# The query blocks of a decoder's channel mixer as products of split halves

## The reference

```python
h   = RMSNorm(x) * (1 + scale2) + shift2
q   = (h @ w_q).reshape(T, 8 heads, 2 halves, 128)
s1  = einsum('thd,nd->thn', q[:, :, 0], key1)      # 128 keys
s2  = einsum('thd,nd->thn', q[:, :, 1], key2)
v1, i1 = top_k(s1, 16) ;  v2, i2 = top_k(s2, 16)
top, sel = top_k(v1[..., :, None] + v2[..., None, :], 16)   # of 256 candidates
# gate = softmax(top); expert ids from i1, i2, sel
act = gelu(h @ u[ids]) ;  x += (1 + gate2) * sum(gate * act * v[ids])
```

## Time and profile before

| | us |
|---|---|
| median of 3 runs (3113.21 to 3117.46) | 3115.37 |
| the profiled execution, its own time | 3108.82 |
| span of the profiled execution | 3106.8 |
| TensorE busy in the span | 2897.8 (93%) |
| VectorE busy | 2318.7 (75%) |
| ScalarE busy | 1109.2 (36%) |
| GpSimd busy | 99.6 (3%) |

### The profile page before, as it was taken

The page is one execution under the profiler, slowest core; times in us unless marked ns, Lnnn a source line. Parts: engine busy times, 40 slices in busy tenths (PEclk is TensorE's granted clock), DMA queues, the critical chain, the costliest instruction groups (busy, mean ns, idle before and its releaser), DMA issues. The chain is left out here.

```text
span 3106.8 us, 49920 instructions
## 1 busy us (share of the span) xinstructions
PE 2897.8 (93%) x19180; PEld 2609.3 (84%) x19180; DVE 2318.7 (75%) x4553; ACT 1109.2 (36%) x1581; POOL 99.6 (3%) x120
## 2 busy tenths in 40 slices
PE   5997998789999999999989989887899999999998
PEld 4996787668999998777789878776799999987776
DVE  7998575558886846888879886555498858488887
ACT  3433321202444444333344332221134444443333
POOL 0000003200000000000000000131000000000000
PEclk8998999989999999999999999999999999999999
DMA  6552340053757598888745425301556585988885
GB/s 264 184 189 82 144 174 10 33 219 136 227 200 244 187 314 308 308 307 303 266 154 182 161 75 203 95 8 63 217 178 230 163 296 167 339 310 307 306 305 217
DMA packets 271007, 627.15 MB, mean 202 GB/s; under 512 B 45616, under 2 KB 210096, under 8 KB 212272
## 3 DMA queue, kind: packets, MB, share of 16 engines
q1 hardware_dynamic: 205168, 590.37, 53.5%
q10 hardware_dynamic: 65600, 33.55, 3.6%
HBM read 554.12 MB, written 69.73 MB: 201 GB/s over the span
## 5 line engine op out<-in xcount | busy, mean ns | idle before, releaser
L899 PE MATMUL ps<-h_hi,u_hi 128*128 128x256 f32 x2048 | 586.8, 287 | 8.3 <-DVE u_lo L1674 8.3
L899 PE MATMUL ps<-h_lo,u_hi 128*128 128x256 f32 x2048 | 579.3, 283 | 0.0
L899 PE MATMUL ps<-h_hi,u_lo 128*128 128x256 f32 x2048 | 579.1, 283 | 0.0
L1674 DVE TENSOR_TENSOR u_lo<-ring,u_hi 128x1024 fp32r<-128x1024 f32 x256 | 312.4, 1221 | 212.4 <-ACT u_hi L1148 212.1
L1167 ACT ACTIVATE v_hi<-ring 128x1024 fp32r<-128x1024 f32 x256 | 271.3, 1061 | 426.9 <-PE ps L920 426.9
L899 PEld LDWEIGHTS ps<-h_hi,u_hi 128*128 128x128 f32 x2048 | 392.7, 192 | 11.1 <-DVE u_lo L1674 10.9
L899 PEld LDWEIGHTS ps<-h_lo,u_hi 128*128 128x128 f32 x2048 | 392.9, 192 | 0.0
L899 PEld LDWEIGHTS ps<-h_hi,u_lo 128*128 128x128 f32 x2048 | 392.6, 192 | 0.0
L1681 DVE TENSOR_TENSOR v_lo<-ring,v_hi 128x1024 fp32r<-128x1024 f32 x256 | 313.0, 1223 | 68.0 <-ACT v_hi L1167 67.2
L920 PE MATMUL ps<-v_hi,w_hi 128*128 128x512 f32 x1024 | 322.8, 396 | 1.2 <-DVE w_lo L1797 1.2
L920 PE MATMUL ps<-v_lo,w_hi 128*128 128x512 f32 x1024 | 321.5, 395 | 0.0
(11 more groups left out here) (302 smaller groups left out, 4278.7 us busy)
## 6 DMA issues: line engine op xcount, KB each, us to landing
ring<-in_stream SPq DMA_DIRECT2D x456, 1024.0 KB, 5.4
act_rows<-region SPq DMA_DIRECT2D x256, 128.0 KB, 5.6
gate_rows<-region ACTq DMA_DIRECT2D x4, 8192.0 KB, 57.1
region<-gate_rows SPq DMA_DIRECT2D x256, 128.0 KB, 4.5
region<-act_rows SPq DMA_DIRECT2D x256, 128.0 KB, 4.7
region<-in_c SPq DMA_DIRECT2D x7, 512.0 KB, 6.1
prm<-in_prm SPq DMA_DIRECT2D x3, 470.0 KB, 6.9
xT<-in_x SPq DMA_DIRECT2D x1, 1024.0 KB, 13.7
```

What stands on the lines that cost most here:

```text
L899: ins = mm(ps[:, c % 4, 0:T], x, y[:, k, :], start=k == 0 and i == 0, stop=k == KD - 1 and i == 2)
L1674: vec.tensor_tensor(u_lo[:, c % U_DEEP, :], ring[:, slot, (c % 2) * D:(c % 2 + 1) * D], u_hi[:, c % U_DEEP, :].bitcast(F32), ALU.subtract) ...
```

## The change

The eight query blocks are made as the input projections are, of three products of split halves.

- `project_query(h)` takes the place of `project(W_Q + h, hT)`: 48 products instead of 16. It waits for the remainder of the block, and in head 0 for `h_hi` at its start and for `h_lo` at its third part.
- ScalarE copies the high half of each block into one of three buffers `wq_hi` (`query_hi`). The one of block 0 stands between the last square and `norm_root(1)`, those of blocks 1 and 2 behind the shift, and that of block h + 3 between the copy of query h and the copy of the key scores of head h - 1.
- VectorE makes the remainders of blocks 0 to 3 (`query_lo`): the first ahead of `modulate(1)`, the others behind `h_lo`. `h_hi` is cast in two halves.
- GpSimd makes the remainders of blocks 4 to 7, each as soon as its high half is there.
- The marks of the stage are moved: TensorE's behind the query blocks, ScalarE's behind the loop over the heads, VectorE's behind the remainders, GpSimd's behind its own.

```diff
@@ -92,6 +92,7 @@
 TAPS_AT_CONV, TAPS_AT_RWKV, TAPS_AT_QK, TAPS_AT_V = 6, 15, 4, 6
 
 
+Q_ON_DVE = 4
 U_DEEP, V_DEEP, ROWS_DEEP = 3, 4, 4
 LO_IN_HEAD = (0, 0, 0, 0, 3, 7, 7, 7)
 LO_IN_TAIL = 20
@@ -314,6 +315,7 @@
         zh_hi, zh_lo = over(hot_at, "zh_hi", 0, KD, T), peer("zh_lo", 28928, KD, T)
         zw_hi, zw_lo = peer("zw_hi", 0, 3, KD, T), over(ring_at, "zw_lo", 0, SLOTS, KD, T)
 
+        wq_hi = [peer(f"wq_hi{i}", off, KD, T) for i, off in enumerate((28672, 30720, 14336))]
         u_hi, u_lo = peer("u_hi", 16384, U_DEEP, D), peer("u_lo", 19456, U_DEEP, D)
         h_hi, h_lo = peer("h_hi", 22528, KD, T), peer("h_lo", 24576, KD, T)
         act_s = view(26624, 4, T)
@@ -352,7 +354,7 @@
                  "red_mm", "kk_squares", "kk_sums", "kk_root", "kk_recip", "kk_spread", "bonus_mm", "pre_ready", "ar_ready", "gn_mm", "gn_root", "zeroed", "lam_sum", "att_squares", "conv_act", "lora_act",
                  "gn_squares", "ln_squares", "bonus_prod", "rwkv_out", "merged_ready", "ln_affine", "decay_sums",
                  "decays", "centred", "zh_hi", "zh_split", "kk_unit",
-                 "zw_hi", "zw_lo")
+                 "zw_hi", "zw_lo", "q_lo")
         late = ("key_mm", "key_read", "route_T", "route_copied", "hot_ready", "gates_mm", "gates_copied",
                 "s_ready", "s_gelu", "top_shifted", "top_exp", "route_ready", "staged", "c_silu", "half_stored", "rest_stored", "u_hi", "u_lo", "v_hi",
                 "v_lo", "w_raw", "w_hi", "w_split", "mixed", "h_split", "next_ada", "loads_past", "early_cleared")
@@ -590,6 +592,24 @@
                         for k in range(KD):
                             x, y = (h[:, k, cols], w[:, k, :]) if token_major else (w[:, k, cols], h[:, k, :])
                             ins = mm(o[:, a, :], x, y, start=k == 0 and i == 0, stop=k == KD - 1 and i == 2)
+                ins.then_inc(used, 1)
+
+            def project_query(h):
+
+                n = W_Q + h
+                if h < Q_ON_DVE:
+                    pe.wait_ge(S["zw_lo"], Z_GATE - Z + h + 1)
+                else:
+                    pe.wait_ge(S["q_lo"], h - Q_ON_DVE + 1)
+                bank_wait(pe, n)
+                o, wh, wl = pair(n), wq_hi[h % 3], zw_lo[:, n % SLOTS]
+                for a in range(2):
+                    cols = slice(a * P, (a + 1) * P)
+                    for i, (w, x) in enumerate(((wh, h_hi), (wl, h_hi), (wh, h_lo))):
+                        if h == 0 and a == 0 and i == 2:
+                            pe.wait_ge(S["h_split"], 3)
+                        for k in range(KD):
+                            ins = mm(o[:, a, :], w[:, k, cols], x[:, k, :], start=k == 0 and i == 0, stop=k == KD - 1 and i == 2)
                 ins.then_inc(used, 1)
 
             def norm_sum(turn, first=0, last=KD):
@@ -869,8 +889,7 @@
                 norm_sum(1, 0, 4)
                 project(W_OUT[3], merged)
                 norm_sum(1, 4, KD)
-                pe.wait_ge(S["h_ready"], 2 * KD)
-                st.mark()
+                pe.wait_ge(S["h_split"], 2)
                 def key_scores(h):
 
                     was_read(pe, W_Q + h)
@@ -884,9 +903,10 @@
                     ins.then_inc(S["key_mm"], 1)
 
                 for h in range(H):
-                    project(W_Q + h, hT)
+                    project_query(h)
                     if h:
                         key_scores(h - 1)
+                st.mark()
                 key_scores(H - 1)
                 def scores(c):
 
@@ -924,7 +944,6 @@
                     if c < CHUNKS - 1:
                         ins.then_inc(S["mixed"], 1)
 
-                pe.wait_ge(S["h_split"], 1)
                 for c in range(CHUNKS):
                     scores(c)
                     if c == ROUTE_AT:
@@ -1136,9 +1155,20 @@
                 for i, n in enumerate(W_OUT):
                     was_read(act, n)
                     square(i)
+                def query_hi(h):
+
+                    if h < H:
+                        n = W_Q + h
+                        landing(act, n)
+                        if h >= 3:
+                            act.wait_ge(used, taken(n - 3))
+                        A(wq_hi[h % 3][:, :, :], blk[n % SLOTS], ACT.Copy).then_inc(S["zw_hi"], 1)
+
+                query_hi(0)
                 norm_root(1)
                 shift(1)
-                st.mark()
+                query_hi(1)
+                query_hi(2)
                 def u_high(c):
 
                     n = PEER + c // 2
@@ -1152,11 +1182,13 @@
                         n = W_Q + h
                         act.wait_ge(used, taken(n))
                         A(q2[:, 2 * h:2 * h + 2, :], pair(n), ACT.Copy).then_inc(bank_read[bank(n)], 1)
+                        query_hi(h + 3)
                     if h:
                         act.wait_ge(S["key_mm"], h)
                         A(scs[:, h - 1, :, :], ps[:, 4 + (h - 1) % 4, :].rearrange("p (a t) -> p a t", a=4), ACT.Copy).then_inc(S["key_read"], 1)
                     if h > H - U_DEEP:
                         u_high(h - H + U_DEEP - 1)
+                st.mark()
 
                 def v_high(c):
 
@@ -1661,11 +1693,22 @@
                     ins.then_inc(bank_read[bank(n)], 1)
                     if i < 3:
                         late_ada(13 + i)
+                def query_lo(h):
+
+                    n = W_Q + h
+                    dve.wait_ge(S["zw_hi"], Z_GATE - Z + h + 1)
+                    vec.tensor_tensor(zw_lo[:, n % SLOTS], blk[n % SLOTS], wq_hi[h % 3][:, :, :].bitcast(F32), ALU.subtract).then_inc(S["zw_lo"], 1)
+
+                query_lo(0)
                 modulate(1)
-                dve.wait_ge(S["h_ready"], 2 * KD)
+                for half in (slice(0, KD // 2), slice(KD // 2, KD)):
+                    dve.wait_ge(S["h_ready"], KD + half.stop)
+                    vec.tensor_copy(h_hi[:, half, :], hT[:, half, :]).then_inc(S["h_split"], 1)
+                dve.wait_ge(S["h_split"], 2)
+                vec.tensor_tensor(h_lo[:, :, :], hT[:, :, :], h_hi[:, :, :].bitcast(F32), ALU.subtract).then_inc(S["h_split"], 1)
+                for h in range(1, Q_ON_DVE):
+                    query_lo(h)
                 st.mark()
-                ch.join(vec.tensor_copy(h_hi[:, :, :], hT[:, :, :]))
-                vec.tensor_tensor(h_lo[:, :, :], hT[:, :, :], h_hi[:, :, :].bitcast(F32), ALU.subtract).then_inc(S["h_split"], 1)
 
                 def u_low(c):
 
@@ -1884,6 +1927,10 @@
                             expand(g, 0)
                             expand(g, 1)
                 st.meet()
+                for h in range(Q_ON_DVE, H):
+                    n = W_Q + h
+                    pool.wait_ge(S["zw_hi"], Z_GATE - Z + h + 1)
+                    gp.tensor_tensor(zw_lo[:, n % SLOTS], blk[n % SLOTS], wq_hi[h % 3][:, :, :].bitcast(F32), ALU.subtract).then_inc(S["q_lo"], 1)
                 st.mark()
                 pool.wait_ge(stage, 4 * st.k)
                 pool.wait_ge(S["loads_past"], 1)
```

## The result

The changed kernel takes 3121.02 us (median of 14 runs, 3115.86 to 3128.49) against 3113.36 (14 runs, 3108.86 to 3118.27) of the kernel before. The ratio is 1.0024, 95% interval 1.0015 to 1.0033: slower by 7.5 us, with an interval from 4.7 to 10.3 (the medians differ by 7.7). The forecast was +9.2.

What follows compares the result with a forecast made beforehand. VectorE's top-k and u_lo up to chunk 3 were taken to bound the kernel, not TensorE's query blocks. Two layers x (2.05 later top-k + 2.5 meeting) = +9.2 us, giving 3124.6 on the median; range 3117 to 3131.

Steps and rivals of the forecast that it cites:

- VectorE sets the end of this stage: Query stage to chunk 3: VectorE's top-k and u_lo set the end, with 0.05 us of slack at chunk 3.
- Cost of the query blocks: TensorE's query blocks: 48 split products take 5.78 us a block instead of 6.91.
- High half and remainder of block 0 ahead of the norm: Before the first query block: reciprocal 2.4 us later, TensorE's first query product 2.95 us later.
- Start of the top-k: VectorE's head 0: the top-k starts 2.05 us later than before in each layer.
- The meeting: GpSimd's remainder 6 lies across head 1's candidate sums on VectorE and holds them 2.5 us a layer; bounds 0 and 5.1.
- Lower clock in front of chunk 0: TensorE's wait before chunk 0: a return to the lower clock costs 1.6 us in chunk 0, hidden by u_lo's pace.
- A sign of being wrong that came: First expert chunks: the prediction is wrong if the first u_lo come with a smaller delay than 4.6 us.
- The other sign: Expert chunk 3 on TensorE: the prediction is wrong if it starts without waiting for u_lo.
- its first rival: Candidate sums: GpSimd doesn't hold VectorE or phases miss; only the later top-k counts, +4.1 us, 3119.5; chance 0.24.
- TensorE's saving: Rival, query blocks: TensorE's shorter work reaches the end, -12.2 us, 3103.2; chance 0.08.
- a GpSimd of 10 us an instruction: Rival, remainders of blocks 4 to 7: slow GpSimd instructions hold VectorE longer, +18 us, 3133; chance 0.12.
- the lower clock: Rival, chunks 0 to 2: the lower clock stays, chunk 3 starts 1.8 us late, +12.8 in all, 3128.2; chance 0.10.

Runs made afterwards that it cites:

- fewer products: Changed kernel without the products of the block's remainder with h_hi in query blocks 5 to 7; ratio 1.0031 against the kernel before.
- GpSimd out of the way: Changed kernel with GpSimd's remainders 5 to 7 held until VectorE has done the candidate sums of heads 0, 1 and 2; ratio 1.0011 against the kernel before.
- root first: Changed kernel with block 0's high half behind norm_root(1) and its remainder behind the halves of h_hi; ratio 1.0023 against the kernel before.
- copy first: Changed kernel with ScalarE's copy of the key scores ahead of the high half of block h + 3; ratio 1.0029 against the kernel before.
- TensorE kept busy: Changed kernel with 20 extra float32 products, whose results nothing reads, ahead of query block 0; ratio 1.0031 against the kernel before.
- three parts: Changed kernel with GpSimd remainders 4, 6, 7 waiting for candidate sums, key scores copied before the next high half, 20 extra products before block 0; ratio 1.0001.
- kernel before, 24 u_lo in a new order: Kernel before with three u_lo moved into head 3, the sum of 24 in the heads kept; ratio 1.0012 against the kernel before.
- changed kernel, the same order: Changed kernel with three u_lo moved into head 3, sum of 24 kept; 3103.73 against 3110.95 us of the kernel before, ratio 0.9974.
- three parts, the same order: The three parts kernel with three u_lo moved into head 3, sum of 24 kept; 3107.42 us, ratio 0.9989 against the kernel before.
- 30 early u_lo: First three u_lo moved to head 3, six more made before the routing: changed kernel 1.0016, kernel before 1.0061, changed kernel with further edits 1.0002.

## Why the prediction was right, step by step

- *VectorE sets the end of this stage.* Shown: the marks of the changed kernel (chunk 3 behind u_lo, 7.96 us of waiting in front of chunk 0), and the run with fewer products, where 5.8 us a layer vanished in the wait.
- *Cost of the query blocks.* 5.78 us expected; from 705.67, where block 1 starts on TensorE, to its key scores at 711.43, 5.76. Block 0, at the lower clock for its first half, took 705.67 - 698.28 = 7.39, where 5.78 + 1.6 was charged.
- *High half and remainder of block 0 ahead of the norm.* +2.4 expected at the reciprocal, +2.2 measured; +2.95 at TensorE's first product, +2.7 measured. The copy took 1.89 us and the remainder 2.29, as in the earlier trace rows.
- *Start of the top-k.* +2.05 expected, +2.00 measured. That ScalarE's high half in front of the key scores is 1.4 of it was shown by the copy put first.
- *GpSimd.* 5.1 us expected, 4.61 measured. This was the term that was mis-sized: I had multiplied the time of a 512-element instruction by four. The Trainium skill's 4497 ns for two inputs of this size (GPSIMD Engine Reference, section 3.1) was nearer. The meeting was forecast with the sums of head 1 and no others, and so it was, 1.9 instead of 2.5 us; of the 0.6, the shorter instruction gives 0.5. It was shown by removing it (-1.9) and by moving it (+1.17 and +1.1, where 1.2 and 1.1 were expected).
- *The Trainium skill's rule on single-input instructions* (SBUF — State Buffer, Who interferes with whom): the trace agrees for MAX8: four of them took 0.87 us beside GpSimd (717.81) and without it (715.00).
- *Lower clock in front of chunk 0.* It came, and it was hidden, as argued. The granted clock was at 0.50 (1.2 GHz) from 757 to 766.6 us, and chunk 0 took 5.15 us (761.72 to 766.87) instead of 2.96, a cost of 2.2 us where 1.6 was charged. u_lo of chunk 1 ended 4.5 us after that of chunk 0, and TensorE still waited 0.77 us in front of chunk 2.
- *The sum.* 2 x (2.0 + 1.9) = 7.8 us on the marks, 9.2 forecast, 7.5 measured.
- *A sign of being wrong that came.* The prediction calls itself wrong if the first u_lo come with a smaller delay than 4.6 us. They came 3.9 later (74.43 against 70.50). The other sign did not come: TensorE starts chunk 3 0.05 us behind its u_lo. So the path held, and the sizes on it were too large: the delay of the first u_lo is the sum of the two terms above, and 0.6 of the missing 0.7 is the meeting.

The absolute time alone would not have told the forecast from its first rival. 3121.0 lies nearer to the 3119.5 of the case without a meeting than to 3124.6, and it is just below the forecast's own range (3122.4 to 3127.2) and below its line for "slower" (3121.6). Some 2 us of this come from the time of the kernel before, which was 3115.37 in three runs and 3113.36 in fourteen. What decides for the forecast is the stretched row and the run without it.

Of the rivals, no meeting and TensorE's saving are excluded by the runs above; a GpSimd of 10 us an instruction did not occur, and the lower clock was gone before chunk 2.

How far the marks carry to the end is the open part. The two profiled executions (3119.65 and 3108.82) differ by 10.8 us, and the second is shorter than all 14 timed runs of its kernel. From chunk 3 to the last chunk the changed kernel takes 430.2 and 428.9 us in the two layers, the kernel before 426.5 and 425.5. That is 7 us more behind the marks, and some 4 us less in the rest of the program. In all the traces with the old order of u_lo this length lies between 425.5 and 431.1, so one execution can't say whether the change is a cause of it. The medians can be set beside the marks, here as differences from the kernel before in us, both layers together. The first gate step is TensorE's first product with `hot`, 210.0 and 211.1 us after the last square in the kernel before.

| kernel | u_lo of chunk 3 | first gate step | time |
|---|---|---|---|
| changed | +7.8 | +9.6 | +7.5 |
| GpSimd out of the way | +4.0 | +4.4 | +3.4 |
| root first | +7.8 | +6.9 | +7.2 |
| copy first | +9.6 | +10.8 | +9.0 |
| fewer products | +7.8 | +7.9 | +9.6 |
| TensorE kept busy | +5.6 | +4.8 | +9.6 |
| three parts | -1.0 | +0.3 | +0.3 |
| kernel before, 24 u_lo in a new order | -1.5 | +4.9 | +3.7 |
| changed kernel, the same order | -12.7 | -6.4 | -8.1 |
| three parts, the same order | -16.4 | -5.1 | -3.4 |

With the order of u_lo left alone, the time follows the mark of chunk 3 within 2 us, but for the run with TensorE kept busy. With a new order that mark no longer tells; the first gate step still does, within 2 us. (The kernels with 30 early u_lo are left out, since their gate step comes six chunks later.)

## What to carry to other kernels

Before an engine's work is made shorter, look at what that engine does next and for whom it waits there: here TensorE had 0.05 us in hand over VectorE, so 18 us of saved TensorE time bought nothing until the order of VectorE's work was moved to meet it, and then the edit that had made the kernel slower made it faster. The work given to GpSimd cost something here only where a VectorE instruction with two SBUF inputs fell into it. With GpSimd instructions of 4.6 us, lay their times against VectorE's, and tie GpSimd's start to VectorE's step rather than to its data. An earlier start of one engine shifts such phases, so price it together with them.

## What the runs showed of the hardware

- A VectorE instruction with two SBUF inputs that meets a GpSimd instruction shows no idle time and no wait; it only looks long (2.63 us for a pair of 0.74). A wait list doesn't find it, a comparison of the same line from head to head does.
- TensorE's granted clock came back some 3.6 us after the start of block 0 in the changed kernel (698.28 to about 701.9, and as long in layer 1). Where the block started earlier, with two short waits between its parts, it came back 9 us after the start in layer 0 (696.33 to 705.2) and 5.7 us in layer 1. What makes the difference is not shown.
